# Attention scores of a three-term float32 product: two terms as one 128-row product a head, the third as two 64-row products side by side

## The chip, the cores and the metric

The kernel runs on one NeuronCore of a Trainium2 chip. The metric is the device time of one execution in microseconds (us), the median of several runs. The profile is of one further execution.

## What is computed

One decoder layer serves a prompt of 1024 tokens and 64 sample tokens (8 sequences of 8, each with 256 cached tokens). The part that the change touches is the attention of the prompt, 8 heads of 64 channels:

```python
z = jnp.einsum('bqhd,bkhd->bhqk', q, k) * (64 ** -0.5) + bias
mask = k_pos < q_pos
later = reverse_cumsum(where(mask, log_sigmoid(-z), 0)) - log_keep
a = where(mask, exp(log_sigmoid(z) + later), 0)
out = einsum('bhqk,bkhd->bqhd', a, v)
```

q, k and v come out of one input projection of 1024 channels to 5120 outputs. Everything is float32.

## The kernel before

A float32 product is made of three products of a fast form (fp32r): each factor is split into a high part h and a rest l, and a*b is taken as ah*bh + ah*bl + al*bh. The high part is what ScalarE writes when it copies a bank of PSUM into an fp32r tile; the rest is the difference, taken by VectorE.

The layer runs in stages on TensorE: the norm and turning of x (about 0 to 40 us), four passes over two heads each (`pair`, to about 650 us), the branches' output projections, the output norm, the up-projection with its convolution, the down-projection, and the end. Only the four passes are touched. Heads 2c and 2c+1 of pass c lie in partitions 0 to 63 and 64 to 127 of the tiles `qh`, `ql`, `kh`, `kl` [128 x 1088 tokens].

A pass begins with nine units of the input projection, three token groups (384, 384 and 320 tokens) each of q, k and v. A unit is 8 x 3 matmuls (L2769, L2770, L2771) into one of two banks that alternate, so a unit's bank has to be emptied while the next unit runs: unit u waits (`drained`) until unit u-2 has been taken out. For q, ScalarE writes `qh` (L1253) and VectorE `ql` (L2008); for k, ScalarE writes a plain copy `kf` (L1257) and `kh` (L1258), and VectorE `kl` (L2008). In pass 0 the units of q and k take turns, and both engines also still split x block by block (`x0_high`, `x0_low`, `x0_scaled`): the order of each engine's queue is written out by hand (`if first:` in both).

Then come 28 slots. One step is one head with 128 queries against up to 512 keys; steps 1 to 24 go through both heads of each query block, in eight blocks of queries (four blocks of queries against the first half of the keys, four against the second half and four against the first again, so 12 blocks a pass). `scores(j)`, at odd slots, makes the scores of two steps, head 0 and head 1. Per query block the key width is 128, 256, 384, 512 (the triangle, twice a pass) and 512 four times. For the first block of each triangle (`opens(j)`) one call makes the scores of two query blocks, widths 128 and 256; so there are 10 calls a pass, two of them openings. Between the scores a slot has the turning of finished weights (L2723), every fourth time the products with v (L2945), and six pieces of the remaining projection units (three matmuls each), with which TensorE fills the time that VectorE and ScalarE need for sigmoid, mask, scan and product.

Each of the three terms of a step uses only 64 of the array's 128 rows. The two heads' products of one term are issued one after the other, on the upper and the lower rows, into different banks.

Of the kernel before, what the change touches and what calls it, by code (L numbers as in the profile page):

```python
# [6 lines left out]
F32R = mybir.dt.float32r  # L7
I32 = mybir.dt.int32
ALU = mybir.AluOpType
ACT = mybir.ActivationFunctionType  # L10
ds = bass.ds

P = 128
D = 1024
KD = D // P
SEQ = 1024
NB, NT = 8, 8
NS = NB * NT
TOK = SEQ + NS
# [38 lines left out]
def step_shape(s):  # L58

    if s == SAMPLE:  # L60
        return PAGES * P + NS, PAGES * P
    qh, c, i, _ = STEPS[s]
    return (P * (i + 1), P * i) if c == qh else (4 * P, None)
# [7 lines left out]
def score_cols(s):  # L71

    o = P if s != SAMPLE and STEPS[s][0] == STEPS[s][1] and STEPS[s][2] == 1 else 0
    return slice(o, o + step_shape(s)[0])
# [118 lines left out]
def build(nc, inp, out, gate_spill, x1_spill, x2_spill, f_spill):  # L193
    with ExitStack() as ctx:
        def sem(name):
            return ctx.enter_context(nc.semaphore(name))
# [4 lines left out]
        def at(name, shape, offset, dt=F32):  # L201
            size = 4
            for x in shape[1:]:
                size *= x
            assert BASE + offset + size <= TOP, (name, offset + size)
            return nc.alloc_sbuf_tensor_at(name, shape, dt, offset=BASE + offset)
# [20 lines left out]
        a = Region(R1, R2)  # L227
# [7 lines left out]
        LOW = 1152 - BASE  # L235
        a = Region(R1, R2)
# [20 lines left out]
        a = Region(R3, RTOP)  # L257
# [21 lines left out]
        x3 = at("x3", [P, D], R3)  # L279

        a = Region(R2 + ACTS, R3)
        qh, kh = a.take("qh", [P, TOK], F32R), a.take("kh", [P, TOK], F32R)
        ql, kl = a.take("ql", [P, TOK], F32R), a.take("kl", [P, TOK], F32R)
        vT = a.take("vT", [P, TOK])
        pk = at("pk", [P, 2, 4, P], a.p - TOK * 4)
        vn = a.take("vn", [P, BLK + 1, P])
# [19 lines left out]
        a = Region(start_at, start_at + 20480)  # L306
# [7 lines left out]
        a = Region(R3T, RTOP)  # L314
# [5 lines left out]
        a = Region(R3T, RTOP)  # L320
# [4 lines left out]
        a = Region(R3T, RTOP)  # L325
# [29 lines left out]
        a = Region(R3T, RTOP)  # L355
# [19 lines left out]
        def f(t):  # L375
            return t.bitcast(F32)
# [64 lines left out]
        sb_ = banks[3:5]  # L441
# [56 lines left out]
        a_qk = sem("a_qk")  # L498
# [19 lines left out]
        d_qk = sem("d_qk")  # L518
# [37 lines left out]
        p_s, p_wT, p_av = (sem(n) for n in ("p_s", "p_wT", "p_av"))  # L556
# [43 lines left out]
        def part(t, g):  # L600

            o, w = GROUPS[g]
            return t[..., o:o + w]
# [15 lines left out]
        def unit_of(j, gr, first):  # L619

            return 2 * gr + j if first and j < 2 else NG * j + gr
# [527 lines left out]
        def _(act):  # L1149
            s_ = nc.scalar  # L1150
# [94 lines left out]
            def pair(c, first, last=False):  # L1245

                def unit_in(j, gr):
                    u = unit_of(j, gr, first)
                    act.wait_ge(p_unit, punit.at(u + 1))
                    return banks[u % 2][:, 0:GROUPS[gr][1]]  # L1250

                def q_high(gr):
                    s_.activation(part(qh[:, :], gr), unit_in(0, gr), ACT.Copy).then_inc(a_qk, 1)  # L1253

                def k_high(gr):
                    b = unit_in(1, gr)
                    s_.activation(part(kf[:, :], gr), b, ACT.Copy).then_inc(a_kv, 1)  # L1257
                    s_.activation(part(kh[:, :], gr), b, ACT.Copy).then_inc(a_qk, 1)  # L1258

                def pages_in(q):  # L1260
                    if q >= 2:
# [43 lines left out]
                def natural(kind, g):  # L1305

                    if kind == 0:
                        act.wait_ge(stg_out[g], stn[g].at())
                        dst = stg[g][:, :].rearrange("p (b n) -> p b n", n=P)
                    else:  # L1310
                        dst = vn[:, 3 * g:3 * g + 3, :]

                    def ops(b):
                        b = b[:, 0:384].rearrange("p (b n) -> p b n", n=P)
                        if g < 2:
                            return [(dst, b)]
                        return [(dst[:, 0:2, :], b[:, 0:2, :]), (dst[0:NS, 2, :], b[0:NS, 2, :])]
                    evac(ops, b=ob_)
                    act.wait_ge(a_m, mis.at())
                    o, os_, sm = (kp_o, ks_o, stg_out[g]) if kind == 0 else (vp_o, vs_o, vn_out)  # L1320
                    nb = 3 if g < 2 else 2
                    act.dma_start(o[:, 3 * g:3 * g + nb, ds(c * P, P)], dst[:, 0:nb, :]).then_inc(sm, 16)
                    if g == 2:
                        act.dma_start(os_[:, ds(c * P, P)], dst[0:NS, 2, :]).then_inc(sm, 16)
                    if kind == 0:
                        stn[g].step(16 if g < 2 else 32)

                for g in range(NG):
                    s_.activation(part(vT[:, :], g), unit_in(2, g), ACT.Copy).then_inc(a_kv, 1)
                    natural(0, g)  # L1330

                def fill(i):

# [20 lines left out]
                for n in range(SLOTS):  # L1354
                    if n < NSTEP:
                        w, masked = step_shape(n)
# [10 lines left out]
                        b, h = sb_[n % 2][:, score_cols(n)], 4 if n == SAMPLE else STEPS[n][3]  # L1367
# [11 lines left out]
                    if 0 <= s < NSTEP:  # L1379
                        act.wait_ge(p_wT, att.at(s + 1))  # L1380
                        b = pb_[s % 2]
                        if s == SAMPLE:
                            s_.activation(aas[0:NS, 0:P], b[0:NS, PAGES * P:(PAGES + 1) * P], ACT.Copy)

                            for r in range(2):
                                dst, src = (t.rearrange("p g (j r x) -> p g j r x", r=2, x=2 * NT)[:, :, :, r, :]
                                            for t in (aasp[:, r, :, :], b[:, 0:PAGES * P].rearrange("p (g n) -> p g n", g=PAGES)))
                                ins = s_.activation(dst, src, ACT.Copy)
                        else:
                            _, _, i, h = STEPS[s]  # L1390
                            w = step_shape(s)[0]
                            if (s - 1) // 4:

                                act.wait_ge(p_av, avn.at(2 * ((s - 1) // 4)))
                            ins = s_.activation(wT[:, h, 0:w // P, i % 2 * P:i % 2 * P + P],
                                                b[:, 0:w].rearrange("p (k n) -> p k n", n=P), ACT.Copy)
# [19 lines left out]
                    if n == SAMPLE_SLOT + 3:  # L1416
# [5 lines left out]
                        for h in range(2):  # L1422
                            rows = slice(64 * h, 64 * h + 64)
                            ins = s_.activation(oT[rows, ds(c, 1), SEQ:TOK].rearrange("p o (b q) -> p (o b) q", q=NT), src[rows, :, h, :], ACT.Copy)
# [486 lines left out]
        def _(dve):  # L1911
            v = nc.vector
# [86 lines left out]
            def pair(c, first, last=False):  # L1999
# [5 lines left out]

                def rest(lo, j, hi, gr):
                    b = unit_in(j, gr)
                    v.tensor_tensor(part(lo[:, :], gr), b, part(f(hi[:, :]), gr), ALU.subtract).then_inc(d_qk, 1)  # L2008

                def q_low(gr):  # L2010
                    dve.wait_ge(a_qk, qkn.step())
                    if gr == NG - 1:
                        new = unit_in(0, gr)[:, SEQ - GROUPS[gr][0]:]
                        for h in range(2):
                            rows = slice(64 * h, 64 * h + 64)
                            x = new[rows, :].rearrange("p (b q) -> p b q", q=NT)
                            v.tensor_copy(qpad[rows, :].rearrange("p (b x) -> p b x", x=P + 16)[:, :, h * NT:h * NT + NT], x)
                            ins = v.tensor_copy(qbd[rows, :, h, :], x)
                        ins.then_inc(d_qbd, 1)
                    rest(ql, 0, qh, gr)  # L2020

                def k_low(gr):
                    dve.wait_ge(a_qk, qkn.step())
                    if gr == NG - 1:
                        v.tensor_copy(ks[:, :], unit_in(1, gr)[:, SEQ - GROUPS[gr][0]:]).then_inc(d_qbd, 1)
                    rest(kl, 1, kh, gr)

                if first:
                    x0_scaled(3, 3, 4)
# [73 lines left out]
                for n in range(SLOTS):  # L2103
                    for j in range(n, n + (4 if opens(n) else 2)) if n % 2 else (n,) if n == SAMPLE else ():
                        if j not in MASKED or n % 2 and opens(n - 2):
                            continue
                        w, o = step_shape(j)
                        b, m = sb_[j % 2][:, score_cols(j)][:, o:w], sfar if j == SAMPLE else far
                        dve.wait_ge(p_s, att.at(n + 4 if opens(n) else j + 1))
                        v.tensor_tensor(b, b, m[:, :], ALU.add).then_inc(d_far, 1)  # L2110
                    if n >= 1 and n - 1 < NSTEP:
                        s = n - 1
                        w = step_shape(s)[0]
                        k, x = keep[s % 2], beta[s % 3][:, 0:w]
                        qh_, ch_, i, h = STEPS[s] if s != SAMPLE else (0, 0, 0, 0)
# [561 lines left out]
        def _(pe):  # L2677
            t_ = nc.tensor
# [60 lines left out]
            def pair(c):  # L2739
# [115 lines left out]
                if first:  # L2855
# [3 lines left out]
                    for i in range(2):  # L2859

                        ins = t_.matmul(banks[i], ones[:, :], grow[:, 512 * i:512 * i + 512], start=True, stop=True)
# [40 lines left out]
                def scores(j):  # L2902

                    qh_, c, i, _ = STEPS[j]
                    pe.wait_ge(a_beta, att.at(j))
                    if j == 1:
                        pe.wait_ge(d_qk, qkn.at(2 * NG - 1))
                    elif qh_ == 1 and c == 1 and i == 0:
                        pe.wait_ge(d_qk, qkn.at(2 * NG))
                    for j_ in (j, j + 2) if opens(j) else (j,):  # L2910
                        q0, k0, w = (4 * qh_ + STEPS[j_][2]) * P, 4 * P * c, step_shape(j_)[0]
                        for n, (q, k) in enumerate(((qh, kh), (qh, kl), (ql, kh))):
                            for h in range(2):
                                rows = slice(64 * h, 64 * h + 64)
                                ins = t_.matmul(sb_[(j + h) % 2][:, score_cols(j_)], q[rows, q0:q0 + P], k[rows, k0:k0 + w],  # L2915
                                                start=(n == 0), stop=(n == 2))
                                if n == 2:
                                    ins.then_inc(p_s, 1)

                def weights_turned(s):  # L2920

# [499 lines left out]
```

## Time and profile before

| | before |
|---|---|
| median of 3 runs | 1692.37 us |
| lowest, highest | 1690.55, 1692.79 us |
| the profiled execution | 1690.61 us |
| its span | 1688.9 us |
| granted TensorE clock, mean | 0.999 of full |
| TensorE busy, VectorE, ScalarE, GpSimd | 99%, 65%, 46%, 19% of the span |
| the four passes | to about 650 us |

The busy time of TensorE counts each matmul to its modelled end, and ends overlap the next start; what a matmul costs a queue of matmuls is read from start to start. In the timeline a line "x2" is two matmuls merged: here the two heads' products. "PEld" is the load of the stationary operand.

### The profile page before, as it was taken

What the parts mean: (1) busy time and instruction counts of PE and PEld (TensorE: products, weight loads), DVE (VectorE), ACT (ScalarE), POOL (GpSimd) and SP (SyncE); (2) the same over time, 40 slices, a digit from 0 to 9 for tenths busy, and PEclk for the clock granted to TensorE, in tenths of its full rate; (3) what the DMA queues carried; (4) which work ended last, traced back from release to release, by engine and by line L of the source; (5) the groups of instructions that cost most, each with busy time, mean ns of one, the idle gap of its engine ahead of it and who ended that gap; (6) DMA issues with size and microseconds to landing.
All of it is one profiled execution on the core that took longest, in us unless ns stands there. A gap on an engine that the chain in (4) does not pass through costs nothing. (4 is left out here: it accounts for less than half of the span.)

```text
span 1688.9 us, 27560 instructions
## 1 busy us (share of the span) xinstructions
PE 1676.6 (99%) x9311; PEld 1464.1 (87%) x9311; DVE 1090.2 (65%) x1588; ACT 779.7 (46%) x1369; POOL 317.7 (19%) x262
## 2 busy tenths in 40 slices
PE   9999999999999999999999999999999999999998
PEld 8989998999899899998888888888888788888886
DVE  6365146325532656647678888888888698776576
ACT  6445234434534353225454444444444444465675
POOL 1000000000000000002356666666664000000000
PEclk9999999999999999999999999999999999999999
DMA  5312221132113124352222222222222852245333
GB/s 176 102 54 69 79 80 57 57 98 67 57 60 95 42 73 153 121 197 101 82 83 80 77 78 78 78 78 78 78 78 77 299 200 82 90 149 186 108 125 118
DMA packets 176600, 170.67 MB, mean 101 GB/s; under 512 B 16207, under 2 KB 144555, under 8 KB 176492
## 3 DMA queue, kind: packets, MB, share of 16 engines
q1 hardware_dynamic: 165546, 164.41, 30.1%
q10 hardware_dynamic: 10946, 4.91, 1.0%
q8 instruction: 57, 0.93, 0.2%
q14 instruction: 51, 0.42, 0.1%
HBM read 129.66 MB, written 39.62 MB: 100 GB/s over the span
## 5 line engine op out<-in xcount | busy, mean ns | idle before, releaser
L2769 PE MATMUL pair<-xh,wh 128*128 128x384 f32 (+1 forms) x952 | 324.8, 341 | 0.0
L2771 PE MATMUL pair<-xh,wl 128*128 128x384 f32 (+1 forms) x952 | 311.1, 327 | 0.0
L2770 PE MATMUL pair<-xl,wh 128*128 128x384 f32 (+1 forms) x952 | 310.5, 326 | 0.0
L2769 PEld LDWEIGHTS pair<-xh,wh 128*128 128x128 f32 x952 | 179.2, 188 | 4.4 <-issue 2.3
L2770 PEld LDWEIGHTS pair<-xl,wh 128*128 128x128 f32 x952 | 179.3, 188 | 0.0
L2771 PEld LDWEIGHTS pair<-xh,wl 128*128 128x128 f32 x952 | 178.7, 188 | 0.0
L1057 POOL TENSOR_TENSOR srow<-hn,hn 128x512 f32<-128x512 f32 x8 | 12.1, 1508 | 811.7 <-DVE hn L2257 811.4
L3293 PE MATMUL pair<-woph,foph 128*128 128x512 f32 x308 | 120.8, 392 | 0.7 <-DVE fopl L2410 0.7
L3295 PE MATMUL pair<-woph,fopl 128*128 128x512 f32 x308 | 120.0, 389 | 0.0
L3294 PE MATMUL pair<-wopl,foph 128*128 128x512 f32 x308 | 119.9, 389 | 0.0
L1368 ACT ACTIVATE keep<-pair,bias 128x512 f32<-128x512 f32 (+4 forms) x100 | 58.2, 582 | 125.8 <-DVE pair L2110 53.6
L1924 DVE TENSOR_TENSOR wl<-raw,wh 128x1024 fp32r<-128x1024 f32 x48 | 58.8, 1224 | 75.3 <-ACT wh L1175 74.9
L1725 ACT ACTIVATE foph<-f 128x512 fp32r<-128x512 f32 x77 | 48.4, 629 | 83.4 <-PE pair L3295 79.6
L2110 DVE TENSOR_TENSOR pair<-pair,far 128x128 f32<-128x128 f32 x64 | 15.1, 294 | 85.9 <-PE pair L2915 85.6
L3293 PEld LDWEIGHTS pair<-woph,foph 128*128 128x128 f32 x308 | 57.8, 188 | 13.9 <-DVE fopl L2410 1.6
L3295 PEld LDWEIGHTS pair<-woph,fopl 128*128 128x128 f32 x308 | 57.8, 188 | 12.2
L3294 PEld LDWEIGHTS pair<-wopl,foph 128*128 128x128 f32 x308 | 57.8, 188 | 11.7
L3137 PE MATMUL pair<-bh,tch 128*128 128x512 f32 x168 | 67.5, 402 | 0.3 <-DVE u L2296 0.3
L3137 PE MATMUL pair<-bh,adh 128*128 128x512 f32 x168 | 65.5, 390 | 0.8 <-DVE uv L2368 0.8
L3139 PE MATMUL pair<-bh,tcl 128*128 128x512 f32 x168 | 65.7, 391 | 0.0
L3138 PE MATMUL pair<-bl,tch 128*128 128x512 f32 x168 | 65.5, 390 | 0.0
L3139 PE MATMUL pair<-bh,adl 128*128 128x512 f32 x168 | 65.4, 389 | 0.0
(407 smaller groups left out, 4262.4 us busy)
## 6 DMA issues: line engine op xcount, KB each, us to landing
rawp<-in_w_up SPq DMA_DIRECT2D x88, 256.0 KB, 3.9
raw<-in_w_in SPq DMA_DIRECT2D x80, 256.0 KB, 3.2
wd<-in_w_down SPq DMA_DIRECT2D x55, 256.0 KB, 3.0
f_spill<-cv SPq DMA_DIRECT2D x22, 552.0 KB, 2.8
f<-f_spill SPq DMA_DIRECT2D x44, 256.0 KB, 5.5
gat<-gate_spill SPq DMA_DIRECT2D x16, 544.0 KB, 4.4
x_spill<-x SPq DMA_DIRECT2D x16, 512.0 KB, 3.0
gate_spill<-stg SPq DMA_DIRECT2D x32, 192.0 KB, 1.9
```

What stands on the lines that cost most here:

```text
L1368: s_.activation(keep[n % 2][:, 4 * P - w:4 * P], b, ACT.Sigmoid, scale=-SCALE, bias=bias2[:, h + 2:h + 3] if n != SAMPLE else bias2[:, 5:6 ...
L1725: s_.activation(fop[s % NFOP][0][:, :], fa[F_OF[n]][k][:, :], ACT.Copy).then_inc(a_fh, 1)
L1924: v.tensor_tensor(wl[s][:, :], raw[s][:, :], f(wh[s][:, :]), ALU.subtract).then_inc(d_lo, 1)
L2769: t_.matmul(b, h, xhi, start=(k == 0), stop=False, skip_group_check=True)
L2770: t_.matmul(b, h, xlo, start=False, stop=False, skip_group_check=True)
L2771: ins = t_.matmul(b, l, xhi, start=False, stop=(k == KD - 1), skip_group_check=True)
L3137: t_.matmul(o, w, x, start=n in "1675" and k == 0, stop=False, skip_group_check=True)
L3138: t_.matmul(o, w, xlow, start=False, stop=False, skip_group_check=True)
L3139: ins = t_.matmul(o, wlow, x, start=False, stop=k == KH - 1, skip_group_check=True)
L3293: t_.matmul(o, xh_[:, cols], w[0][:, :], start=n in (0, 2, 3, 5) and k == 0, stop=False, skip_group_check=True)
L3294: t_.matmul(o, xh_[:, cols], w[1][:, :], start=False, stop=False, skip_group_check=True)
L3295: ins = t_.matmul(o, xl_[:, cols], w[0][:, :], start=False, stop=k == KF - 1, skip_group_check=True)
```

## The change

Before, a step had six products on 64 rows, three for each head. Now head h has tiles of its own: `qs[h]` holds the head's q high part in its own 64 partitions and its q rest in the other 64; `ks2[h]` holds the head's k high part twice, in both halves. One product over all 128 rows, `qs[h]` with `ks2[h]`, gives qh*kh + ql*kh. The third term qh*kl stays a product on the head's own 64 rows, the two heads one after the other. The scores of two steps are so 2 products on 128 rows and 2 on 64, where there were 6 on 64.

ScalarE writes the high parts of q and k in two instructions of 64 partitions in place of one of 128, and doubles the keys (`k_twice`, two copies of 64 x 1024) after the first v unit of each pass. VectorE takes each rest in two instructions of 64 partitions in place of one of 128. `kl` moves to another address. Transfers are as before.

```diff
-        qh, kh = a.take("qh", [P, TOK], F32R), a.take("kh", [P, TOK], F32R)
-        ql, kl = a.take("ql", [P, TOK], F32R), a.take("kl", [P, TOK], F32R)
+        qs = [a.take(f"qs{h}", [P, TOK], F32R) for h in range(2)]
+        ks2 = [a.take(f"ks2{h}", [P, TOK], F32R) for h in range(2)]
+        kl = at("kl", [P, TOK], LOW, F32R)
+        def own(h):
+            return slice(64 * h, 64 * h + 64)
+        def other(h):
+            return slice(64 - 64 * h, 128 - 64 * h)
...
                 def q_high(gr):
-                    s_.activation(part(qh[:, :], gr), unit_in(0, gr), ACT.Copy).then_inc(a_qk, 1)
+                    b = unit_in(0, gr)
+                    for h in range(2):
+                        ins = s_.activation(part(qs[h][own(h), :], gr), b[own(h), :], ACT.Copy)
+                    ins.then_inc(a_qk, 1)
...
-                    s_.activation(part(kh[:, :], gr), b, ACT.Copy).then_inc(a_qk, 1)
+                    for h in range(2):
+                        ins = s_.activation(part(ks2[h][own(h), :], gr), b[own(h), :], ACT.Copy)
+                    ins.then_inc(a_qk, 1)
+                def k_twice():
+                    for h in range(2):
+                        s_.activation(ks2[h][other(h), 0:SEQ], f(ks2[h])[own(h), 0:SEQ], ACT.Copy)
...
                     natural(0, g)
+                    if g == 0:
+                        k_twice()
...
                 def rest(lo, j, hi, gr):
                     b = unit_in(j, gr)
-                    v.tensor_tensor(part(lo[:, :], gr), b, part(f(hi[:, :]), gr), ALU.subtract).then_inc(d_qk, 1)
+                    for h in range(2):
+                        ins = v.tensor_tensor(part(lo(h), gr), b[own(h), :], part(f(hi[h])[own(h), :], gr), ALU.subtract)
+                    ins.then_inc(d_qk, 1)
...
-                    rest(ql, 0, qh, gr)
+                    rest(lambda h: qs[h][other(h), :], 0, qs, gr)
...
-                    rest(kl, 1, kh, gr)
+                    rest(lambda h: kl[own(h), :], 1, ks2, gr)
...
-                        for n, (q, k) in enumerate(((qh, kh), (qh, kl), (ql, kh))):
-                            for h in range(2):
-                                rows = slice(64 * h, 64 * h + 64)
-                                ins = t_.matmul(sb_[(j + h) % 2][:, score_cols(j_)], q[rows, q0:q0 + P], k[rows, k0:k0 + w],
-                                                start=(n == 0), stop=(n == 2))
-                                if n == 2:
-                                    ins.then_inc(p_s, 1)
+                        for h in range(2):
+                            t_.matmul(sb_[(j + h) % 2][:, score_cols(j_)], qs[h][:, q0:q0 + P], ks2[h][:, k0:k0 + w], start=True, stop=False)
+                        for h in range(2):
+                            t_.matmul(sb_[(j + h) % 2][:, score_cols(j_)], qs[h][own(h), q0:q0 + P], kl[own(h), k0:k0 + w],
+                                      start=False, stop=True).then_inc(p_s, 1)
```

## Rows read from the trace of the kernel before

**Rows 1.** The page: TensorE's busy time, and the chain that ended last by engine.
```profile
PE 1676.6 (99%) x9311; PEld 1464.1 (87%) x9311; DVE 1090.2 (65%) x1588; ACT 779.7 (46%) x1369; POOL 317.7 (19%) x262
...
PE 46%; DVE 1%; issue 0%; DVEq 0%; ACT 0%
```

**Rows 2.** Waits of the weight loads, whole span: us in total, times, longest.
```profile
PEld pair L2915 <- issue: 8.7, 40, 0.3
```

**Rows 3.** Timeline of TensorE at one call of width 512: start, duration (us).
```profile
89.02 0.31 PE L2770 MATMUL pair<-xl,wh 128*128 128x320 f32 x1
89.16 0.31 PE L2771 MATMUL pair<-xh,wl 128*128 128x320 f32 x1
89.40 0.50 PE L2915 MATMUL pair<-kh,qh 64*128 64x512 f32 x2
89.74 0.39 PE L2915 MATMUL pair<-kl,qh 64*128 64x512 f32 x2
89.97 0.40 PE L2915 MATMUL pair<-kh,ql 64*128 64x512 f32 x2
```

**Rows 4.** Timeline of TensorE at an opening, widths 128 and 256.
```profile
68.20 0.27 PE L2915 MATMUL pair<-kl,qh 64*128 64x128 f32 x2
68.31 0.27 PE L2915 MATMUL pair<-kh,ql 64*128 64x128 f32 x2
...
68.59 0.29 PE L2915 MATMUL pair<-kl,qh 64*128 64x256 f32 x2
68.71 0.28 PE L2915 MATMUL pair<-kh,ql 64*128 64x256 f32 x2
68.93 0.45 PE L2769 MATMUL pair<-xh,wh 128*128 128x384 f32 x1
69.21 0.34 PE L2770 MATMUL pair<-xl,wh 128*128 128x384 f32 x1
69.39 0.35 PE L2771 MATMUL pair<-xh,wl 128*128 128x384 f32 x1
```

**Rows 5.** Timeline of TensorE: full products of widths 128 and 512.
```profile
14.92 0.28 PE L2797 MATMUL pair<-xh,wh 128*128 128x128 f32 x1
15.03 0.28 PE L2798 MATMUL pair<-xl,wh 128*128 128x128 f32 x1
...
890.32 0.39 PE L3137 MATMUL pair<-sop2h,adh 128*128 128x512 f32 x1
890.55 0.39 PE L3138 MATMUL pair<-sop2l,adh 128*128 128x512 f32 x1
```

**Rows 6.** Timeline of DVE and PEld in pass 0's head, 26 to 33 us.
```profile
26.20 0.55 DVE L2008 TENSOR_TENSOR ql<-pair,qh 128x384 fp32r<-128x384 f32 x1
26.66 2.63 DVE L1960 TENSOR_TENSOR xl<-pair,xh 128x512 fp32r<-128x512 f32 x4
...
30.29 0.56 DVE L2008 TENSOR_TENSOR kl<-pair,kh 128x384 fp32r<-128x384 f32 x1 [0.99 <-ACT kh L1258]
...
29.41 0.13 PEld L2723 LDWEIGHTS pair<-ident,cwr 19*128 19x128 f32 x1 [0.39 <-issue]
32.89 0.20 PEld L2723 LDWEIGHTS pair<-ident,xn 128*128 128x128 f32 x2 [0.23 <-DVE xn L1952]
```

**Rows 7.** Timeline of PEld at slot 15 of pass 1.
```profile
256.73 0.42 PEld L2723 LDWEIGHTS pair<-ident,beta 128*128 128x128 f32 x4 [0.45 <-DVE beta L2127]
```

**Rows 8.** Timeline of DVE and ACT in pass 1: q units, a v unit.
```profile
183.19 0.56 DVE L2008 TENSOR_TENSOR ql<-pair,qh 128x384 fp32r<-128x384 f32 x1 [2.41 <-ACT qh L1253]
...
186.73 0.49 ACT L1253 ACTIVATE qh<-pair 128x384 fp32r<-128x384 f32 x1 [3.67 <-PE pair L2771]
...
213.27 0.49 ACT L1329 ACTIVATE vT<-pair 128x384 f32<-128x384 f32 x1 [3.63 <-PE pair L2771]
```

**Rows 9.** ScalarE on 1024 columns: the timeline, and groups (us, mean ns).
```profile
22.95 1.05 ACT L1206 ACTIVATE junk<-xlast 64x1024 bf16<-64x1024 f32 x1
...
L1175 ACT ACTIVATE wh<-raw 128x1024 fp32r<-128x1024 f32 x43 | 45.6, 1061 | 0.0
```

## The prediction

> **What bounds the kernel now.** I read the page first. TensorE is busy for 99% of the span, and the chain that ended last is TensorE with next to nothing of another engine [rows 1]. So a microsecond more or less of TensorE's own queue goes into the time whole, and work of VectorE or ScalarE counts only where TensorE stands still for it. The second view is therefore the timeline of TensorE in the passes, from start to start. A full product of 384 columns follows the last after 0.18 us at 69.21 (0.17 in the long run), one of 512 after 0.23, one of 128 after 0.11 [rows 4, 5]. Steps above these values are the places where time is lost. I went through all starts to 660 us for them. Apart from the places around the scores and other products on part of the array, there are few: in the head of pass 0 [rows 6], at slot 15 of passes 1 and 2 [rows 7], and one of some 0.3 us in slot 0 or 1 of passes 1 to 3. The third view is the list of waits: the weight loads of the scores stood idle before 40 calls for 8.7 us with "issue" as the cause, 0.22 us a call [rows 2]. The fourth is the timeline of ScalarE and VectorE where q and k are taken out.
>
> **The slots of the scores.** Two heads' 64-row products of one term are one line "x2": they start together, and the next term follows after 0.23 us for 512 columns, 0.12 for 256, 0.11 for 128 [rows 3, 4]. A full 128-row product takes the same slot: 0.23 us for 512, 0.11 for 128 [rows 5]. A call of today is three slots (three side-by-side pairs). The new one is a slot for head 0's full product, one for head 1's, one for the pair of the third term: three slots again. The half-empty array of today is not idle time, because the other head fills it; six matmuls become four, but not one column streams less. For all 48 query blocks (4 passes x two of 128, 256, 384 and six of 512) a slot sum is 4 x (2 x 0.11 + 2 x 0.12 + 2 x 0.17 + 6 x 0.23) = 8.7 us, and it is three of these, 26 us, before and after. Difference 0, at most 0.1 us either way for the rounding.
>
> **The change between 128 and 64 rows.** This is the term that decides. Going in: the 320-column product at 89.16 should hold the queue 0.14 us (89.02 to 89.16), but the scores start after 0.24, and the second term comes 0.34 after the first where the slot is 0.23 [rows 3]. So 0.10 + 0.11 = 0.21 us are lost: the load does not run ahead under the previous product, as it does between full products. Coming out without another wait, at the first opening: 68.71 to 68.93 is 0.22 where 256 columns take 0.12, and the first full product holds 0.28 where 0.18 is right: 0.10 + 0.10 = 0.20 us [rows 4]. A round trip costs 0.41 us. Today there is one in each of 40 calls. In the new kernel the two full products come first, in the same form as the projection before them, so going in costs nothing there; but the step from full to half now lies inside the call, before the third term, and the way out stays. In 32 of 40 calls the loss is only moved. In the 8 openings the loop over j_ makes full, half, full, half: one round trip more each. 8 x 0.41 = +3.3 us. From both sides: nothing below if both changes could be hidden, the 0.20 of one side alone gives 1.6; above, 0.6 a trip (both sides a half dearer) gives 4.8. No row shows a full-to-half step without a semaphore wait before it; the way out at 68.93, which has none, is the nearest and costs 0.20. So I take 3.3.
>
> The Trainium skill, "TensorEngine Tiling (Array Packing)", section Key Properties, says that a change of tiling mode, though not a change of tile, drains TensorE, without a figure. By that rule, with the prices of the rows, the sum is the same +3.3; without a drain it would be the first rival's.
>
> Of these 3.3 us something is given back. At slot 15 of passes 1 and 2, just behind the second opening, TensorE waited 0.3 us over its slot for VectorE's weights (0.45 of the loads' idle time) [rows 7]. VectorE's chain there is fed by earlier scores and is not lengthened by this opening, so TensorE, arriving 0.4 later, waits 0.3 less: 2 x 0.3 = -0.6 (from 0 to -0.6). The 0.3 us in slot 0 or 1 wait for a copy of ScalarE that itself follows TensorE, so they stay.
>
> **The head of pass 0.** VectorE's second instruction of each rest costs about 0.46 us in its queue (26.20 to 26.66; 0.56 if it ran alone), ScalarE's second high part 0.4 (an estimate, from 0.49 alone) to 0.49 [rows 6, 8]. I give 64 partitions the time of 128, as the columns set it: ScalarE takes 1.05 us for 64x1024 and 1.06 for 128x1024 [rows 9]. In front of the convolution rows' turn at 29.41 the loads are idle for 0.39 us: TensorE waits for `x0_low(5)`, the end of the run that starts at 26.66 and ends 29.29, right behind `q_low(0)`. One more VectorE instruction there is +0.46. Then k: `kl` waits for `kh` and starts at 30.29; with a second high part and a second rest VectorE is free for `x0_scaled(6)` 0.4 + 0.46 = 0.86 us later, up to 1.05. TensorE already waits for that block's `xn` at 32.89 [rows 6], 0.23 in all. It arrives 0.46 later by itself, and the block is ready 0.86 later: another 0.4. Together +0.9 us, between 0.46 (only the first) and 1.05. Behind that the timeline has over a microsecond of slack for the last x rests.
>
> **Work that is hidden.** In the later passes the rest of a q unit is done at 183.75, and the next unit is ready only at 186.73, after ScalarE was idle for 3.67 us [rows 8]. Of the 3.0 us between, the change takes 0.4 + 0.5. A unit of 24 products of 0.17 lasts 4.2 us; taking it out grows from 1.2 to 2.1. A k unit has a ScalarE copy more: 2.5 of 4.2. `k_twice` is 2 x 1.06 us [rows 9] and lies in ScalarE's wait of 3.63 us for the second v unit [rows 8]; the DMA issue of 0.4 us ahead of it still leaves 0.9. Behind it are queued only that v copy and the natural-layout copies; TensorE asks for the doubled keys 10 us later. If this cover were gone, 24 ScalarE copies of 0.4, 24 VectorE ones of 0.5 and 8.5 us of `k_twice` would cost some 30 us, but no row makes any of it late. The masks start when all the scores of a call are done, as today; with the opening 0.4 longer, they and the steps behind shift with TensorE. Cost 0, at most 0.5.
>
> **Sum.** 0 + 3.3 - 0.6 + 0.9 = +3.6 us on the profiled execution: 1690.6 to 1694.2. The median shown is 1.76 us above the profiled one, so the median to expect is 1692.4 + 3.6 = 1696.0 us. About 0.2%, 3.4 us, is what a measurement can tell from no change, and the sum lies on that line.
>
> **The rivals.**
> - *The step from full to half is free inside a call.* Today's 0.21 us stands behind a wait on a semaphore in all 40 calls. Were it the wait, or a load for 64 rows that could run ahead when nothing is waited for, 40 x 0.21 = 8.4 us would vanish, 8 x 0.20 = 1.6 more ways out come, and 0.9 of the head: -5.9 us, 1686.5. Against it: the waits before the projection's units (`drained`) and before L2723 cost no gap where they are already met, and the way out at 68.93 has no wait at all and still costs 0.20 [rows 4]. For it stands the sentence of "TensorE: Matmul & The Clock Gate", Part 2, of the Trainium skill, that TensorE pulls weight loads ahead when row groups don't conflict or when they go to a background buffer; for a change of rows no run here shows that. This is the case on the other side; it turns the sign once a full-to-half step costs under about 0.12 us. Chance 0.1.
> - *The opening's extra trip is paid, but more of it is taken up* (shorter waits of TensorE behind it, 0.2 for the second switch), and the head gives only 0.46: +1.5 to 2.5 us, 1694.5. Chance 0.2.
> - *Taking out q and k becomes late in passes 1 to 3*, because the pages' copies and the weight splitting stand in the same queues: TensorE waits in front of the units. It decides once a unit's removal passes 4.2 us; one such wait of 1 us a pass gives +3 more, 1699. The 2.1 and 2.5 us above speak against. Chance 0.1.
> - *The third term's two products no longer run side by side* (the change does not do what it says): one slot sum more, +8.7, 1704.7. They keep form, order and banks. Chance 0.03.
>
> **How the numbers follow.** My forecast, +2.5 to +5, has 0.57. The range for 8 in 10 runs from 1691.5 to 1699: up to a late unit a pass, down to the second rival's lower end (1.5) and the scatter of a median, 2 us. Half of the forecast's own chance falls on each side of 3.4 us, a little more above: slower 0.33 + 0.12 of the last two, same 0.24 + 0.18 + 0.04; faster 0.09 of the first rival.
>
> **What would show it.** In the new timeline: the full scores follow the projection after its plain slot (0.14 or 0.17); three slots of 0.23; a loss of 0.2 in front of and within the 64-row pair; at openings two such losses, together 0.4 us more than now; the list of waits with 48 idle loads in front of the 64-row products in place of 40. The conv rows' turn about 0.46 later and the turn of block 6 about 0.9 later than now. Slots 15 of passes 1 and 2 nearly without wait. It is wrong if loads of the third term start under the full products, if the pair of the third term costs two slots, or if a wait for ql, kl or `ks2` appears in front of a projection unit.

## The result, and the profile after

| | before | after |
|---|---|---|
| median of 12 runs each | 1690.74 us | 1694.07 us |
| lowest, highest | 1690.46, 1692.79 | 1693.20, 1697.61 |
| ratio of the times, 95% interval | | 1.0021, 1.0014 to 1.0028 |
| the profiled execution, its span | 1690.61, 1688.9 | 1693.81, 1692.1 |

The change costs 3.3 us, 0.2%. The median before is 1.6 us lower over twelve runs than over the first three, so the difference of 3.6 us that was forecast, not the 1696.0, is what the measured 3.3 us is to be held against.

The page of the changed kernel, its chain by engine, and the first waits of the weight loads for the scores (us in total, times, longest), answer to [rows 1, 2]:

```profile
PE 1678.1 (99%) x9215; PEld 1466.3 (87%) x9215; DVE 1103.8 (65%) x1612; ACT 800.4 (47%) x1401; POOL 317.7 (19%) x262
...
PE 46%; DVE 1%; issue 0%; DVEq 0%; ACT 0%
...
PEld pair L2938 <- issue: 10.8, 32, 0.4
```

TensorE has 96 matmuls fewer and is busy 1.5 us longer. The idle loads now stand in front of L2938, the third term on 64 rows; the full products (L2936) have none. The list counts 32 stretches and not the 48 that I had named: in front of the 16 blocks of widths 128 and 256 the loads stand idle too, but only for 0.07 and 0.13 us, and the list leaves such short stretches out.

A call of width 512 on TensorE after, start and duration, answering to [rows 3]:

```profile
90.93 0.31 PE L2793 MATMUL pair<-xl,wh 128*128 128x320 f32 x1
91.08 0.31 PE L2794 MATMUL pair<-xh,wl 128*128 128x320 f32 x1
91.23 0.63 PE L2936 MATMUL pair<-ks,qs 128*128 128x512 f32 x2
91.78 0.49 PE L2938 MATMUL pair<-kl,qs 64*128 64x512 f32 x2
92.21 0.87 PE L2966 MATMUL pair<-wT,vn 128*64 128x256 f32 x8
```

The scores follow the projection after 0.15 us, its plain slot, where it had been 0.24. From the last projection matmul to the products with v it is 92.21 - 91.08 = 1.13 us. In the kernel before, the same way took 1.13 us:

```profile
89.16 0.31 PE L2771 MATMUL pair<-xh,wl 128*128 128x320 f32 x1
...
90.29 0.87 PE L2945 MATMUL pair<-wT,vn 128*64 128x256 f32 x8
```

The two full products take 0.55 in place of 2 x 0.23 = 0.46: the 0.1 us in front of the change of rows has moved to this place, and nothing is gained or lost.

The first opening after, answering to [rows 4], from the last three turns of v (one line) to the first full product behind it:

```profile
69.26 0.49 PE L2746 MATMUL pair<-ident,vT 128*128 128x128 f32 x3
69.51 0.42 PE L2936 MATMUL pair<-ks,qs 128*128 128x128 f32 x2
69.86 0.33 PE L2938 MATMUL pair<-kl,qs 64*128 64x128 f32 x2
70.11 0.50 PE L2936 MATMUL pair<-ks,qs 128*128 128x256 f32 x2
70.54 0.38 PE L2938 MATMUL pair<-kl,qs 64*128 64x256 f32 x2
70.86 0.45 PE L2792 MATMUL pair<-xh,wh 128*128 128x384 f32 x1
```

From 69.26 to 70.86 is 1.60 us. Before, the same way began here and ended with the projection at 68.93, after 1.31 us:

```profile
67.62 0.49 PE L2723 MATMUL pair<-ident,vT 128*128 128x128 f32 x3
```

So an opening costs 0.29 us more. All eight do, within 0.01 us, and each of the other 32 calls takes what it took before, within 0.01 us.

The head of pass 0 (ScalarE, VectorE and the weight loads), answering to [rows 6]:

```profile
22.93 0.98 ACT L1265 ACTIVATE qs<-pair 64x384 fp32r<-64x384 f32 x2 [0.48 <-PE pair L2822]
23.94 1.06 ACT L1216 ACTIVATE junk<-xlast 64x1024 bf16<-64x1024 f32 x1
...
25.75 1.29 DVE L1981 TENSOR_TENSOR xl<-pair,xh 128x512 fp32r<-128x512 f32 x2 [0.30 <-ACT xh L1229]
27.07 1.12 DVE L2030 TENSOR_TENSOR qs<-pair,qs 64x384 fp32r<-64x384 f32 x2
28.23 2.48 DVE L1981 TENSOR_TENSOR xl<-pair,xh 128x512 fp32r<-128x512 f32 x4
...
31.16 1.12 DVE L2030 TENSOR_TENSOR kl<-pair,ks 64x384 fp32r<-64x384 f32 x2 [0.45 <-ACT ks L1272]
...
30.83 0.13 PEld L2746 LDWEIGHTS pair<-ident,cwr 19*128 19x128 f32 x1 [1.42 <-issue]
34.45 0.85 PEld L2746 LDWEIGHTS pair<-ident,xn 128*128 128x128 f32 x8 [0.36 <-DVE xn L1973]
```

The loads before the convolution rows' turn are idle for 1.42 us, where it was 0.39. One rest held VectorE's queue for 0.46 us before (26.20 to 26.66); the two of 64 partitions hold it for 1.16 (27.07 to 28.23). On ScalarE the two high parts of q hold it for 1.01 us (22.93 to 23.94), where the single one held it for 0.39, up to the 22.95 of [rows 9]:

```profile
22.56 0.49 ACT L1253 ACTIVATE qh<-pair 128x384 fp32r<-128x384 f32 x1 [0.47 <-PE pair L2799]
```

Going through the starts of TensorE in both timelines, matmul for matmul, gives the whole account of the profiled pair. Each figure is by how much the lag of the changed kernel grows: 0.37 us before the first unit is taken out, with nothing changed there; 1.04 at the convolution rows' turn, 0.15 at block 6, 0.10 at the sample's pages; then 0.29 at each of the 8 openings, 2.3 together; -0.32 behind slot 15 of each of passes 1 and 2; and -0.1 in sum of small steps both ways. Together 3.2 us, the difference of the spans. The 0.37 us is scatter and not the change: the first product behind it starts at 19.39 us before and 19.75 after, and at 19.3 to 20.1 in the traces of the experiments below. What the change itself does adds up to 2.9 us. At slot 15 of pass 1 the loads of [rows 7] no longer wait:

```profile
259.15 0.42 PEld L2746 LDWEIGHTS pair<-ident,beta 128*128 128x128 f32 x4
```

### The profile page after: what moved, and what is told of

Its sections match the earlier page's. It is cut to its first block and busy times, and to the rows that moved or that the text cites. A ratio compares the mean times of both kernels' runs of the same rounds, so it can differ in the third digit from the quotient of the medians.

```text
span 1692.1 us, 27424 instructions
## 1 busy us (share of the span) xinstructions
PE 1678.1 (99%) x9215; PEld 1466.3 (87%) x9215; DVE 1103.8 (65%) x1612; ACT 800.4 (47%) x1401; POOL 317.7 (19%) x262
```

## The experiments

Each was timed beside the kernel before, and its difference is of medians against that kernel's on the same chip (1690.35, 1690.39 or 1690.60 us). The changed kernel was not timed again with them: what is said to be over or under it is the difference of such a difference and its 3.3 us, uncertain by one to two us. Where such a step is small, it is the trace that shows it.

**The openings grouped (e1_group).** One round trip per call again, all else as changed.

```diff
-                    for j_ in (j, j + 2) if opens(j) else (j,):
+                    for j_ in of:            # of = (j, j + 2) at an opening, else (j,)
                         for h in range(2):
                             t_.matmul(... qs[h][:, q0:q0 + P], ks2[h][:, k0:k0 + w], start=True, stop=False)
+                    for j_ in of:
                         for h in range(2):
                             t_.matmul(... qs[h][own(h), q0:q0 + P], kl[own(h), k0:k0 + w], start=False, stop=True)
```

> The changed kernel, but at an opening all four full products come first and then the four of the third term (widths 128 and 256), so each call has one way from 128 to 64 rows and back, as before the change. Theory A (the openings' second round trip costs 0.29 us each, 8 of them, less 0.6 us given back at slot 15): 1.7 us less than the changed kernel, so 1.6 us over the kernel before, what is left being the head of pass 0. Rival B (the loss is not the switching but the added ScalarE and VectorE instructions): the same as the changed kernel, 3.3 us over the kernel before.

Measured 1692.28 us, +1.9; ratio 1.0011 (1.0002 to 1.0020). The first opening:

```profile
69.17 0.49 PE L2746 MATMUL pair<-ident,vT 128*128 128x128 f32 x3
69.41 0.71 PE L2937 MATMUL pair<-ks,qs 128*128 128x128 f32 x4
70.05 0.50 PE L2942 MATMUL pair<-kl,qs 64*128 64x128 f32 x4
70.48 0.45 PE L2792 MATMUL pair<-xh,wh 128*128 128x384 f32 x1
```

69.17 to 70.48 is 1.31 us, what it was before the change. The second round trip of the openings is 1.60 - 1.31 = 0.29 us, and taking it away gives 1.4 us of the 3.3 back (1.7 expected). By the clock alone this would not be certain, as the interval of the ratio overlaps that of the changed kernel. The traces show it: all eight openings are 0.29 us shorter than in the changed kernel, and at slot 15 of passes 1 and 2 TensorE waits 0.25 us longer again, which leaves 1.8. Theory A holds, and rival B, which wanted no difference, falls.

**Only the copies (e2_copies).** The kernel before with q_high, k_high and rest in halves.

```diff
-                    s_.activation(part(qh[:, :], gr), unit_in(0, gr), ACT.Copy).then_inc(a_qk, 1)
+                    b = unit_in(0, gr)
+                    for h in range(2):
+                        rows = slice(64 * h, 64 * h + 64)
+                        ins = s_.activation(part(qh[rows, :], gr), b[rows, :], ACT.Copy)
+                    ins.then_inc(a_qk, 1)
...
-                    v.tensor_tensor(part(lo[:, :], gr), b, part(f(hi[:, :]), gr), ALU.subtract).then_inc(d_qk, 1)
+                    for h in range(2):
+                        rows = slice(64 * h, 64 * h + 64)
+                        ins = v.tensor_tensor(part(lo[rows, :], gr), b[rows, :], part(f(hi[rows, :]), gr), ALU.subtract)
+                    ins.then_inc(d_qk, 1)
```

> The kernel before, scores untouched, but with the high parts of q and k and both rests taken in two instructions of 64 partitions each. Theory A: only the head of pass 0 pays, about +1.3 us as the changed kernel's timeline has it (the prediction had 0.9). Rival B: the passes pay too, and all of the 3.3 us is here. Rival C: nothing, and the head's 1.3 us is scatter of the first transfers.

Measured 1691.80 us, +1.45; ratio 1.0011 (1.0002 to 1.0020). Matmul for matmul the lag grows by 0.92 at the convolution rows' turn, 0.25 at block 6 and 0.10 at the pages, and then stays within 0.2 us through all four passes. So this is a cost of the head alone, as theory A has it.

**ScalarE's halves alone, VectorE's halves alone (e7_scalar, e8_vector).** Each the half of e2's edit.

> The kernel before with only ScalarE's high parts of q and k in two instructions of 64 partitions; the rests in one. Theory A (ScalarE is ahead of VectorE in the head; the first extra instruction delays the x split by 0.3, the second delays kl and the scaling by 0.5): +0.5 us over the kernel before. Rival (ScalarE's part is the whole of the 1.4 us): +1.4.

> The kernel before with only VectorE's rests of q and k in two instructions of 64 partitions; the high parts in one. Theory A (VectorE's queue is what TensorE waits for at the turn of the convolution rows and at block 6; a second instruction costs 0.7 there, not 0.46, since two of them don't overlap): +0.7 to +0.9 us over the kernel before. Rival (ScalarE's part is the whole): 0.

Measured +0.7 us (1691.10; ratio 1.0004, 0.9995 to 1.0013) and +0.8 us (1691.23; ratio 1.0006, 0.9997 to 1.0015). Both intervals hold 1, so the two single values are not certain by the clock; their sum of 1.5 us agrees with e2. In the timelines the lag over the kernel before grows, at the same three places, by 0.24, 0.28 and 0.09 us with ScalarE's halves (behind a stretch at a lower clock, see the last section) and by 0.53, 0.18 and nothing with VectorE's: 1.3 us in sum, as in e2. Neither engine has the whole.

**More behind the doubling of the keys (e3_twice).**

```diff
                     for h in range(2):
                         s_.activation(ks2[h][other(h), 0:SEQ], f(ks2[h])[own(h), 0:SEQ], ACT.Copy)
+                    for h in range(2):
+                        s_.activation(spare[other(h), :], f(ks2[h])[own(h), 0:SEQ], ACT.Copy)
```

> The changed kernel with two more ScalarE copies of 64x1024 behind the doubling of the keys in each pass (into a spare tile that nobody reads), so 4.2 us where the wait for the second v unit leaves 3.6. Theory: hidden, since TensorE asks for that v unit's bank only a unit (4.2 us) later; within 0.3 us of the changed kernel. Rival (the doubling already sits at the edge): each pass loses 1 to 2 us, 4 to 8 us over the changed kernel.

Measured 1693.63 us, +3.3, the same as the changed kernel's 3.3: the added copies are hidden, and so are the two of the change. From the first unit to the end of the passes the lag between the two kernels' matmuls stays the same within 0.1 us. In the changed kernel's ScalarE timeline of pass 1 the doubling leaves 0.83 us of the wait of [rows 8]:

```profile
212.47 2.13 ACT L1277 ACTIVATE ks<-ks 64x1024 fp32r<-64x1024 f32 x2 [0.67 <-ACT stg L1199]
215.43 0.49 ACT L1348 ACTIVATE vT<-pair 128x384 f32<-128x384 f32 x1 [0.83 <-PE pair L2794]
```

**One more round trip at width 256 (e4_halves).** Blocks of width 512 in two parts.

```diff
+                        n = 2 if w == 4 * P else 1
+                        for p in range(n):
+                            a0, w_ = p * w // n, w // n
                             for h in range(2):
-                                t_.matmul(... ks2[h][:, k0:k0 + w] ...)
+                                t_.matmul(... ks2[h][:, k0 + a0:k0 + a0 + w_] ...)
                             for h in range(2):
-                                t_.matmul(... kl[own(h), k0:k0 + w] ...)
+                                t_.matmul(... kl[own(h), k0 + a0:k0 + a0 + w_] ...)
```

> The changed kernel with each of the 24 query blocks of width 512 made in two parts of 256 columns (full, full, the pair on 64 rows, then the same again): one more round trip between 128 and 64 rows at widths of 256, and 0.01 us of longer slots. Theory A (the 0.29 of an opening is small only because at width 128 a slot is as long as a weight load, so the exposed load is not extra there): 0.41 + 0.01 each, 10 us over the changed kernel. Rival B (a round trip costs 0.29 at any width): 7 us. Rival C (the switch is free when nothing is waited for): under 1 us.

Measured 1702.86 us, +12.5, so 9.2 over the changed kernel; ratio 1.0074 (1.0059 to 1.0090). 9.2 / 24 = 0.38 us for each; in the trace a block of width 512 takes 0.39 to 0.41 us more, 9.8 together. The first such block:

```profile
92.55 0.40 PE L2940 MATMUL pair<-ks,qs 128*128 128x256 f32 x2
92.88 0.39 PE L2942 MATMUL pair<-kl,qs 64*128 64x256 f32 x2
93.19 0.50 PE L2940 MATMUL pair<-ks,qs 128*128 128x256 f32 x2
93.63 0.38 PE L2942 MATMUL pair<-kl,qs 64*128 64x256 f32 x2
93.94 0.44 PE L2972 MATMUL pair<-wT,vn 128*64 128x256 f32 x2
```

It takes 93.94 - 92.55 = 1.39 us against 0.98 (91.23 to 92.21) for the same block in one part. Less 0.03 for three slots that are 0.01 longer, a round trip at this width costs 0.38 us, near the 0.41 of the prediction; rival C, the free switch, is far away.

**An opening without width 128 (e10_wide).** The first block of each opening 256 columns wide, its second half overwritten by the next block.

```diff
+                        w = 2 * P if w == P else w
```

> The changed kernel with the first block of each opening 256 columns wide in place of 128 (128 more columns of scores, later overwritten and never read). Theory A (the second round trip at an opening costs only 0.29 us because a slot of width 128 is as long as a weight load, and a load that is exposed is already in it): the opening's extra trip is then 0.38, plus 3 slots longer by 0.01: 0.12 more at each of 8 openings, 1.0 us over the changed kernel, 4.3 over the kernel before. Rival B (the trip costs 0.29 at openings for another reason): 0.2 us over the changed kernel, 3.5 over the kernel before.

Measured 1694.96 us, +4.4, so 1.0 over the changed kernel; ratio 1.0026 (1.0016 to 1.0036). The first opening:

```profile
68.83 0.49 PE L2746 MATMUL pair<-ident,vT 128*128 128x128 f32 x3
69.08 0.48 PE L2942 MATMUL pair<-ks,qs 128*128 128x256 f32 x2
69.49 0.38 PE L2944 MATMUL pair<-kl,qs 64*128 64x256 f32 x2
69.81 0.51 PE L2942 MATMUL pair<-ks,qs 128*128 128x256 f32 x2
70.24 0.38 PE L2944 MATMUL pair<-kl,qs 64*128 64x256 f32 x2
70.56 0.44 PE L2792 MATMUL pair<-xh,wh 128*128 128x384 f32 x1
```

1.73 us against 1.60, and the same 0.12 to 0.13 more at each of the eight. That makes 1.0 us, which the clock alone could not tell from rival B's 0.2. The pair of the third term holds the queue for 0.32 us at width 256 (69.49 to 69.81) and for 0.25 at 128 (69.86 to 70.11 in the changed kernel), 0.07 apart, where their plain slots differ only by 0.01. This fits theory A, by which at width 128 the slot is the load's and not the product's: it is 0.11 us, against 0.12 at twice the columns and 0.17 at three times, and two loads in a row start 0.11 us apart as well (70.85 and 70.96 behind this opening in the changed kernel). Once the loads are exposed, the short product then adds less than its slot. That the width decides is shown; that the load is the reason is read from these figures and was not tried by itself.

**The two heads' third terms apart (e5_apart).**

```diff
                         for h in range(2):
                             t_.matmul(... qs[h][:, q0:q0 + P], ks2[h][:, k0:k0 + w], start=True, stop=False)
-                        for h in range(2):
                             t_.matmul(... qs[h][own(h), q0:q0 + P], kl[own(h), k0:k0 + w], start=False, stop=True)
```

> The changed kernel with the two heads' third terms no longer side by side: full product of head 0, its third term on 64 rows, full product of head 1, its third term. Theory A (two 64-row products next to each other share one slot, and each step between 128 and 64 rows costs its 0.2): 48 more slots in all, 8.7 us, and 48 more round trips at 0.29 to 0.4, 14 to 19 us; together 23 to 28 us over the changed kernel. Rival (the pair in the changed kernel doesn't share a slot, so only the round trips are new): 14 to 19 us.

Measured 1720.52 us, +30.1, so 26.8 over the changed kernel; ratio 1.0180 (1.0164 to 1.0195), in theory A's 23 to 28 and above the rival's 19. With round trips at 0.38 and 0.29 us the new 48 cost at most 18.2 us, and the rest of at least 8.6 is the 8.7 us of a fourth slot: in the changed kernel the pair shares one. The first call of width 512:

```profile
92.57 0.40 PE L2936 MATMUL pair<-ks,qs 128*128 128x512 f32 x1
92.89 0.49 PE L2937 MATMUL pair<-kl,qs 64*128 64x512 f32 x1
93.32 0.50 PE L2936 MATMUL pair<-ks,qs 128*128 128x512 f32 x1
93.75 0.49 PE L2937 MATMUL pair<-kl,qs 64*128 64x512 f32 x1
94.17 0.87 PE L2965 MATMUL pair<-wT,vn 128*64 128x256 f32 x8
```

It takes 1.60 us where it took 0.98: 0.62 more, a slot of 0.23 and a round trip of 0.39. Each opening takes 0.90 us more and each call of width 384 0.56. Over all 40 calls that is 26.6 us, what the clock has.

**The third term on 128 rows as well (e6_full).** kl in a tile for each head, zero in the other half.

```diff
-        kl = at("kl", [P, TOK], LOW, F32R)
+        klz = [at(f"klz{h}", [P, TOK], LOW + TOK * 4 * h, F32R) for h in range(2)]
...
-                            t_.matmul(... qs[h][own(h), q0:q0 + P], kl[own(h), k0:k0 + w], ...)
+                            t_.matmul(... qs[h][:, q0:q0 + P], klz[h][:, k0:k0 + w], ...)
```

> The changed kernel with the third term on 128 rows too: kl has a tile for each head whose other 64 partitions are zero (set once at the start), so a call is four full products and never changes the rows. Theory A (a round trip of 0.41 us a call is dearer than a fourth slot of 0.11 to 0.23): against the kernel before, each pass saves 2 x (0.41 - 0.23) at the openings, 2 x (0.41 - 0.17) at width 384, 6 x (0.41 - 0.23) at 512, less 0.2 in the 4 calls behind which the products with v change the form anyway: 1.1 us a pass, 4.5 in all; with 1.4 of the head, 3 us less than the kernel before, 6 less than the changed one. Rival B (the switch isn't saved, as something else causes the gaps): 48 more slots, 8.7 us over the changed kernel, 12 over the kernel before.

Measured 1690.01 us, -0.4; ratio 0.9999 (0.9990 to 1.0008). It is level with the kernel before and 3.7 us under the changed kernel: rival B (+12) falls, but of the 6 us that theory A gave over the changed kernel only 3.7 came. The width-512 call in front of the products with v:

```profile
90.19 0.31 PE L2796 MATMUL pair<-xh,wl 128*128 128x320 f32 x1
90.34 0.62 PE L2939 MATMUL pair<-ks,qs 128*128 128x512 f32 x2
90.80 0.62 PE L2939 MATMUL pair<-klz,qs 128*128 128x512 f32 x2
91.35 0.87 PE L2968 MATMUL pair<-wT,vn 128*64 128x256 f32 x8
```

It takes 1.16 us from 90.19, 0.03 more than before: a change of form is still paid on the way to the products on 64 columns. The other calls of width 512 save 0.12 us and not 0.18, those of width 384 0.18 and not 0.24: these calls have a turn behind them, and the way out into a turn costs less than one into the projection. The two openings of a pass show it side by side, 0.17 saved in front of the projection and 0.12 in front of a turn. At slot 15 of each pass 0.1 us is given back, as TensorE arrives earlier than VectorE is done. Per pass 0.7 us are saved, not 1.1, and 1.3 were lost in the head.

**The head as before, the later passes in four full products (e9_mixed).**

```diff
+                        if first:
+                            ... the six products on 64 rows with qh, ql, kh, kl, as before the change
+                            continue
                         for t, (kt) in enumerate((ks2, klz)):
```

> Pass 0 exactly as in the kernel before (64-row products, one instruction for each high part and rest, no doubled keys), passes 1 to 3 as in e6_full (four full products a call). Theory A (e6_full gained about 0.7 us a pass at the calls and lost 1.4 us in the head of pass 0 alone): the head's loss is gone and 3 passes gain, 2 us less than the kernel before. Rival B (e6_full is level because nothing is gained at the calls): level with the kernel before.

Measured 1689.48 us, -1.1; ratio 0.9994 (0.9985 to 1.0003). Its profiled span is 1.8 us shorter than that of before, and the steps by which it gains are the calls of passes 1 to 3. This fits theory A's 2 us, but the interval holds 1: that it beats the kernel before is seen in the trace and not shown by the clock. It does beat the changed kernel, whose interval begins at 1.0014.

## Why the prediction was right, point by point

The measured +3.3 us lies in the forecast of +2.5 to +5, and 1694.07 us in the range of 1691.5 to 1699. The 1696.0 us was 1.9 too high, 1.6 of it from the median of three runs on which it was built.

**The slots: right.** Three slots before and after. A call of width 512 takes 1.13 us in both kernels, and e5_apart shows that the pair in it shares a slot. Merging two terms on half the rows into one full product saves nothing, since the other head filled the array already.

**The change between 128 and 64 rows: the mechanism right, the size too large.** Only the openings pay again; e1_group shows it by taking that trip away. The term was 8 x 0.41 = 3.3 us, and measured it is 8 x 0.29 = 2.3. The step that failed is the addition of 0.21 and 0.20, read at widths of 256 and more, for a block of width 128 as well, where less is lost. e4_halves, e5_apart and e10_wide show the price: 0.38 to 0.39 at width 256 and more, 0.29 where one of the blocks has width 128. The Trainium skill, "TensorEngine Tiling (Array Packing)", section Key Properties, says that changing the tiling mode drains TensorE. This trace agrees in so far as full to half has its price inside a call, with no wait in front of it (91.23 to 91.78, 0.55 in place of 0.46); that a drain is what costs the time no run shows.

**The free switch (first rival): wrong.** It wanted -5.9 us, with the third term's loads running under the full products. These loads stand idle for 10.8 us in the list of waits, and under this rival e4_halves would have cost less than 1 us, where it cost 9.2.

**What is given back at slot 15: right,** -0.6 forecast, -0.64 in the trace. Next to nothing more is taken up behind the openings, and the head gave 1.3 us and not 0.46, so the second rival falls as well.

**The head of pass 0: right in place, too small.** Forecast 0.9 (0.46 to 1.05), measured 1.3 in the trace and 1.45 in e2_copies. The step that failed is the price of the second instruction, taken from the next start of a single one (0.46 on VectorE, 0.4 on ScalarE). Two of 64 partitions hold VectorE's queue for 1.16 us, 0.70 more, and ScalarE's for 1.01, 0.62 more. ScalarE's part was counted only for k; it also makes the split of block 3 late at q, where VectorE then waits 0.30 us. So the convolution rows' turn comes 1.04 us later and not 0.46; in return block 6 adds only 0.15 to that and not 0.4, and 0.10 at the sample's pages was not forecast at all.

**The hidden work: right.** e3_twice shows it for the doubling of the keys, e2_copies for the copies of passes 1 to 3. The rival of late units had no part.

The two errors of size had opposite signs: the openings cost 1.0 us less than forecast, the head 0.4 more. The sum of 3.6 came close to 3.3 partly for that reason, which is luck. With the measured sizes it is 2.3 - 0.6 + 1.3, some 2.9 us. The lowest of the twelve runs of each kernel differ by 2.7; what makes the medians 0.4 us more than the terms no run settles.

## What to carry to other kernels

Count side-by-side products on half the rows as one slot before merging them into a full one: fewer instructions are no gain when the array's rows were all in use. Count instead how often a stretch of TensorE's queue goes from one form to another, at about 0.4 us a round trip here (0.29 where a block is only 128 wide), and group products of one form; a fourth full product on padded zeros can be cheaper than a third one in another form. Splitting a copy by partitions more than doubled its time in the engine's queue here, and where that engine's queue is written out to the last half microsecond, as in a kernel's head, TensorE waits for it.

## What the runs showed that was not expected

**A lower clock behind a slack start.** The changed kernel's runs scatter up to 1697.6 us. Of the four above 1695, three have a mean granted clock of 0.997 or 0.998, where the others have 0.999 or 1.0. The profiled run of e7_scalar is of this kind. Its stretches from 15 to 25 us (busy time and instructions of TensorE, its loads, VectorE, ScalarE and GpSimd, then granted clock, DMA share and GB/s):

```profile
15.00:20.00 5.00, 3.01 (x28) 2.77 (x26) 2.35 (x4) 3.95 (x7) 0.00 (x0) 1.00 0.91 298
20.00:25.00 5.00, 4.94 (x27) 4.95 (x28) 4.72 (x8) 2.98 (x8) 0.00 (x0) 0.66 0.06 17
```

TensorE was busy for only 3.0 of the 5 us from 15 to 20, where the kernel before has 4.5, and in the next 5 us the granted clock averages 0.66, a part of them at 1.2 and not 2.4 GHz. Products of 256 columns follow each other there after 0.21 us in place of 0.12. The span is 1691.2 us where the median run would give some 1689.4. The profiled run of e4_halves shows the same, 3.2 us busy and then a clock of 0.66, and is 1.9 us above the median of its kernel. That the slack start brings the lower clock is read from these two traces; no run tried it.

**Two instructions on 64 partitions overlap less than one with its successor.** VectorE's single rest of 0.55 us lets the next instruction start after 0.46; two of 64 partitions take 1.12 us and let it start after 1.16. In the changed kernel the second of the two starts at 27.64, when the first has ended (27.62), and the next instruction at 28.23, when the second has (28.20); ScalarE's queue shows the same at 23.42 and 23.94. So each half takes the time of the whole, and neither overlaps with its neighbour. The halves differ from their neighbours in the partitions at which they start; whether it is this that keeps them apart was not tried.
